# First layer: modulation by feature tiles, and four projection tiles accumulated in four banks as its weights arrive

## What is computed

```python
shift_l, scale_l, gate_l = jnp.split(jax.nn.silu(c) @ w_mod + b_mod, 3, axis=-1)
shift_c, scale_c, gate_c = jnp.split(jax.nn.silu(c_ctx) @ w_mod + b_mod, 3, axis=-1)
u_lat = rmsnorm(h_lat, norms[layer]) * (1 + scale_l[:, None]) + shift_l[:, None]
u_ctx = rmsnorm(h_ctx, norms[layer]) * (1 + scale_c) + shift_c
...
cq, ckv, k_rope, mq, mk, mv, mo, gates, z = split_cols(u @ w_in, EVEN_SPLITS)
```

## Time and profile before

| what | us |
|---|---|
| median of three timed runs | 4002.68 |
| lowest and highest of them | 4002.27, 4006.74 |
| the profiled execution | 3993.9 |
| its span, first to last instruction | 3992.1 |
| PE busy in the span | 3902.0 |
| DVE, ACT, POOL busy | 1857.0, 975.5, 933.2 |
| mean granted TensorE clock | 0.993 |

### The profile page before, as it was taken

The page is one execution under the profiler, slowest core; times in us unless marked ns, Lnnn a source line. Parts: engine busy times, 40 slices in busy tenths (PEclk is TensorE's granted clock), DMA queues, the critical chain, the costliest instruction groups (busy, mean ns, idle before and its releaser), DMA issues. The chain is left out here.

```text
span 3992.1 us, 48487 instructions
## 1 busy us (share of the span) xinstructions
PE 3902.0 (98%) x18394; PEld 2416.5 (61%) x18394; DVE 1857.0 (47%) x3855; ACT 975.5 (24%) x1838; POOL 933.2 (23%) x992
## 2 busy tenths in 40 slices
PE   7999999999999999989999999999999999999998
PEld 3688997777558468567544565656544444444447
DVE  3227775676343366746466322222566452223134
ACT  4223332333124311145325311111123010000000
POOL 0005775001111111133222111122232122222223
PEclk9999999999999999999999999999999999999999
DMA  5320003111211121132131112113243211111113
GB/s 215 129 89 10 8 9 68 42 47 48 90 35 69 50 64 49 59 110 80 64 98 50 57 37 80 42 58 103 96 139 130 79 32 42 47 48 43 42 45 104
DMA packets 113718, 270.25 MB, mean 68 GB/s; under 512 B 15624, under 2 KB 45178, under 8 KB 112399
## 3 DMA queue, kind: packets, MB, share of 16 engines
q1 hardware_dynamic: 106512, 251.81, 19.1%
q0 software_dynamic: 5920, 13.25, 1.3%
q10 hardware_dynamic: 1056, 2.10, 0.1%
HBM read 218.53 MB, written 50.87 MB: 67 GB/s over the span
## 5 line engine op out<-in xcount | busy, mean ns | idle before, releaser
L426 PE MATMUL upper_banks<-sbuf 128*128 128x512 f32 (+1 forms) x2016 | 771.5, 545 | 1.5 <-issue 1.1
L3325 PE MATMUL upper_banks<-sbuf 128*128 128x512 f32 x1400 | 613.7, 594 | 4.7 <-ACT sbuf L3602 3.1
L426 PEld LDWEIGHTS upper_banks<-sbuf 128*128 128x128 f32 x2016 | 382.4, 190 | 388.8 <-issue 373.5
L3325 PEld LDWEIGHTS upper_banks<-sbuf 128*128 128x128 f32 x1400 | 262.1, 190 | 315.1 <-issue 306.8
L2467 PE MATMUL gla_prod<-sbuf 128*128 128x512 f32 x560 | 247.6, 593 | 0.3 <-DVE sbuf L2499 0.3
L582 DVE TENSOR_TENSOR sbuf<-upper_banks,sbuf 128x512 f32<-128x512 f32 (+1 forms) x140 | 82.0, 586 | 283.1 <-PE upper_banks L426 282.5
L378 POOL TENSOR_TENSOR sbuf<-sbuf 128x512 f32<-128x512 f32 x36 | 47.1, 1307 | 655.5 <-DMA sbuf<-in_w_mlp_out 307.4
L2467 PEld LDWEIGHTS gla_prod<-sbuf 128*128 128x128 f32 x560 | 104.5, 192 | 119.9 <-issue 117.4
L1007 PE MATMUL mla_banks<-sbuf 128*128 128x128 f32 x1344 | 174.3, 278 | 2.5 <-DVE sbuf L1314 1.7
L1627 PE MATMUL mls_banks<-sbuf 128*128 128x512 f32 x392 | 175.1, 593 | 0.0
L1007 PEld LDWEIGHTS mla_banks<-sbuf 128*128 128x128 f32 x1344 | 162.1, 193 | 11.8 <-POOL sbuf L850 7.4
(11 more groups left out here) (569 smaller groups left out, 6635.7 us busy)
## 6 DMA issues: line engine op xcount, KB each, us to landing
sbuf<-in_l_w_in SPq DMA_DIRECT2D x59, 512.0 KB, 4.0
sbuf<-in_w_in SPq DMA_DIRECT2D x52, 512.0 KB, 4.2
sbuf<-in_w_mlp_out SPq DMA_DIRECT2D x40, 512.0 KB, 3.6
sbuf<-in_w_mlp_in SPq DMA_DIRECT2D x32, 512.0 KB, 3.6
sbuf<-in_l_w_mod SPq DMA_DIRECT2D x24, 512.0 KB, 5.2
scratch_gates<-sbuf SPq DMA_DIRECT2D x48, 256.0 KB, 2.0
sbuf<-in_l_w_mod SPq DMA_DIRECT2D x8, 1024.0 KB, 15.3
sbuf<-in_l_w_out SPq DMA_DIRECT2D x16, 512.0 KB, 4.1
```

What stands on the lines that cost most here:

```text
L426: last = nc.tensor.matmul(bank_of(n, c)[:, 0:wd], lw[:, k * P:(k + 1) * P], right_operand(c, base, tw, k, o, wd, to), start=k == 0 and c i ...
L3325: last = nc.tensor.matmul(pb, lw[:, k * P:(k + 1) * P], rhs, start=k == 0 and c in ("P1", "P2", "P5"), stop=k == 3, skip_group_check=True)
```

## The change

1. The modulation weights are cut in another way: column tile c holds 256 columns of shift and the 256 columns of scale for the same feature tiles 2c and 2c+1. So mod and gain of two feature tiles are complete after each column tile (`modulate(c)`).
2. SP loads two projection tiles before column tile 1 and two more before column tile 2 (t1, ckv0, ckv1, cq0), and H's late parts at the end.
3. In `modulation` ACT shifts feature tiles 0 to 5 (EARLY = 6) of the first third, and PE accumulates their products for four projection tiles in banks 0 to 3, between the column tiles. Feature tiles 6 and 7 are added in `mla_block` (chunks 0 to 3). The banks are now one tensor for both blocks.
4. The squares of the second third no longer start in `modulation`; all 16 late squares are in `mla_block`, with the evictions of chunks 0 and 1 in their middle. `late_sums` stands in chunk 2, ahead of its first matmul, `late_spread` in chunk 3 ahead of its last.
5. `mla_stream` is reordered: four tiles on the first third, then t1 and ckv0 by thirds, ckv1 and cq0, then the rest; the mod tiles start later and are denser.

```diff
-        w_next = [Memory.whole[0:P, base + i * D:base + (i + 1) * D] for i in range(2)]
+        w_next = [Memory.whole[0:P, base + i * D:base + (i + 1) * D] for i in range(4)]
...
             for c in range(NC):
...
+                if c < 2:
+                    load_first(2 * c)
+                    load_first(2 * c + 1)
...
-            act.wait_ge(h_late[0], 16)
-            for k in range(4):
...
+            for k in range(EARLY):
+                act.wait_ge(moded, k // 2 + 1)
+                act.wait_ge(lifted, k + 1)
+                for a, n, v in halves_of(0, 512):
+                    last = nc.scalar.activation(U[:, k, a:a + n], U[:, k, a:a + n], ACT.Identity, bias=mod[:, k, v:v + 1],
+                                                scale=gain[:, k, v:v + 1])
+                last.then_inc(normed, 1)
...
+            def products(kk, tiles):
+                pe.wait_ge(normed, kk + 1)
+                for t in tiles:
+                    if kk == 0:
+                        pe.wait_ge(w_first[t], 16)
+                    nc.tensor.matmul(banks[:, t, :], w_next[t][:, kk * P:(kk + 1) * P], U[:, kk, 0:512], start=kk == 0, stop=False)
+
+            pe.wait_ge(silued, 1)
+            columns(0)
+            pe.wait_ge(added, KD - 1)
+            pe.wait_ge(const_in, 48)
+            column_sums(nc, stat, total, ones, range(4)).then_inc(ssum, 1)
+            turn(0)
+            pe.wait_ge(rinvd, 1)
+            spread(nc, factor, rcol, ident, range(4)).then_inc(spreaded, 1)
+            for c in range(1, NC):
+                columns(c)
+                products(2 * c - 2, range(2))
+                turn(c)
+                products(2 * c - 1, range(2))
+                if c > 1:
+                    for kk in range(0 if c == 2 else 4, 2 * c):
+                        products(kk, range(2, 4))
...
             for k in range(1, KD):
                 add(k)
-            copy(1)
+            copy(0)
             dve.wait_ge(rooted, 1)
             nc.vector.reciprocal(rcol[:, 0:4], rcol[:, 0:4]).then_inc(rinvd, 1)
-            copy(2)
+            dve.wait_ge(in_sem, 64)
+            modulate(0)
             dve.wait_ge(spreaded, 1)
...
+            for k in range(5):
+                lift(k)
+            copy(1)
+            for k in range(5, KD):
+                lift(k)
+            modulate(1)
+            for c in range(2, NC):
+                copy(c)
+                modulate(c)
...
-        while m < 32 and ring >= (1 if m < 2 else 3 + 27 * (m // 2) // 16):
+        while m < 32 and ring >= (4 + 4 * (m // 2) if m < 4 else 12 + 17 * (m // 2 - 2) // 14):
...
-        late = [(512, 512, 4 + i) for i in range(4)] + [(1024, 256, i) for i in range(8)]
+        late = [(o, wd, i) for o, wd in thirds()[1:] for i in range(KD)]
+        adds_to = [sum(kk > 0 for _, _, kk in late[:i + 1]) for i in range(len(late))]
...
-                    for kk in range(KD):
+                    for kk in range(EARLY if n < 4 else 0, KD):
                         if t == 0:
-                            pe.wait_ge(normed, KD * (o // 512) + kk + 1)
+                            pe.wait_ge(normed, KD * (o // 512) + kk + 1 - EARLY)
+                        if n == 2 and kk == EARLY:
+                            late_sums()
+                        if n == 3 and kk == KD - 1:
+                            late_spread()
...
             def late_sums():
-                pe.wait_ge(hadd, 11)
+                pe.wait_ge(hadd, adds_to[-1])
...
             shift(0)
-            for i in range(12):
+            for i in range(len(late)):
                 o, wd, kk = late[i]
-                act.wait_ge(h_late[1 if o == 512 else 2], 16)
-                if i >= 2:
-                    act.wait_ge(hadd, i - 1 - (i - 2 >= 4))
-                nc.scalar.activation(hs[:, i % 2, 0:wd] if o == 512 or kk else total[:, o:o + wd], H[:, kk, o:o + wd],
-                                     ACT.Square).then_inc(hsq, 1)
...
+                act.wait_ge(h_late[2 if o == 1024 else kk // 4], 16)
+                if i >= 3:
+                    act.wait_ge(hadd, adds_to[i - 2])
+                nc.scalar.activation(hs[:, i % 2, 0:wd] if kk else total[:, o:o + wd], H[:, kk, o:o + wd], ACT.Square).then_inc(hsq, 1)
+                if i == KD - 1:
+                    evict(0)
+                    evict(1)
```

More of the change, by code:

```diff
@@ L126, in halves_of, with modulation @@
     return [(0, NCTX, 1), (NCTX, w - NCTX, 0)] if o == 0 else [(o, w, 0)]
-def modulation(nc, name, io, mod, gain, U, H, rcol, ones, ident, eps, at, h_late, w_first):
+EARLY = 6
+def modulation(nc, name, io, mod, gain, U, H, rcol, ones, ident, eps, at, h_late, w_first, banks):
     NC = NB = 4
@@ L192, in _, with columns @@
             nc.scalar.activation(rcol[:, 0:4], stat[:, 0:4], ACT.Sqrt, bias=eps, scale=1.0 / D).then_inc(rooted, 1)
-            act.wait_ge(h_late[0], 16)
-            for k in range(4):
[L195 to L199, removed]
+            for k in range(EARLY):
[5 more added lines that the diff above has]
+                last.then_inc(normed, 1)
         @block.tensor
         def _(pe):
[L203 to L210, removed]
+            def columns(c):
                 if c >= 2:
@@ L218, in _, with turn @@
                 last.then_inc(mm_done, 1)
[L219 to L228, removed]
+            def turn(c):
+                pe.wait_ge(copied, c + 1)
+                for a in range(4):
+                    last = nc.tensor.matmul(col[:, 4 * c + a, :], part[:, c % 2, a * P:(a + 1) * P], sel[:], start=True, stop=True)
+                last.then_inc(turned, 1)
+            def products(kk, tiles):
[20 more added lines that the diff above has]
+                        products(kk, range(2, 4))
         @block.vector
@@ L796, in _ @@
             sp.dma_start(tab[64:P, :], io["rope"]).then_inc(tab_in, 16)
-            for t in range(2, NW - 1):
+            for t in range(4, NW - 1):
                 load_w(t)
@@ L942, in _ @@
                     chunk(n)
[L943 to L946, removed]
                 if o == 1024 and (what, j) == ("cq", 1):
@@ L1112, in shift @@
                 o, wd = thirds()[c]
-                for k in range(KD):
+                for k in range(0 if c else EARLY, KD):
                     if c:
@@ L1139, in _ @@
                     nc.scalar.activation(rcol[:, 4:TT], banks[:, 5, 260:256 + TT], ACT.Sqrt, bias=eps, scale=1.0 / D).then_inc(hroot, 1)
+                if n >= 2 and (what != "mod" or j % 2):
+                    evict(n)
+                if n == 2:
+                    shift(1)
+                    act.wait_ge(zeroed, 1)
+                    act.wait_ge(misc_in, 16 * 9)
+                    nc.scalar.activation(sc[:, :, 0:2], cc.rearrange("p (a b) -> p a b", b=2), ACT.Silu).then_inc(silued, 1)
                 if n == 3:
-                    shift(1)
                     shift(2)
@@ L1272, in _ @@
             last.then_inc(zeroed, 1)
-            for i in range(12):
+            for i in range(len(late)):
                 o, wd, kk = late[i]
-                if i == 4:
+                if kk == 0:
                     continue
@@ L4826, in lower_layers @@
         mod, mod1, gain = s.sb("mod", [P, 3 * KD, 2]), s.sb("mod1", [P, 3 * KD, 2]), s.sb("gain", [P, KD, 2])
-        h_late, w_first = [s.sem(f"h_late{i}") for i in range(3)], [s.sem(f"w_first{i}") for i in range(2)]
-        modulation(nc, "mod0", io, mod, gain, U, H, rcol, ones[:], ident[:], eps[:], 7680, h_late, w_first)
+        h_late, w_first = [s.sem(f"h_late{i}") for i in range(3)], [s.sem(f"w_first{i}") for i in range(4)]
+        first = ExitStack()
+        banks = first.enter_context(nc.psum_tensor("mla_banks", [P, 8, 512], F32))
+        modulation(nc, "mod0", io, mod, gain, U, H, rcol, ones[:], ident[:], eps[:], 7680, h_late, w_first, banks)
         mv, ma, mn, mf, ao = scratch("mv", [T, 512]), scratch("ma", [8, T]), scratch("mn", [8, T]), scratch("mf", [8, T]), scratch("ao", [512, T])
         ahead, ahead_at = [s.sem(f"ahead{i}") for i in range(2)], Memory.top + KV_WEIGHTS
-        o_out = mla_block(nc, "mla", U, H, io, mv, ma, mn, mf, ao, mod, gain, rcol, mod1, ones, ident, eps[:], ahead, h_late, w_first)
+        o_out = mla_block(nc, "mla", U, H, io, mv, ma, mn, mf, ao, mod, gain, rcol, mod1, ones, ident, eps[:], ahead, h_late, w_first, banks)
+        first.close()
         retire_semaphores()
```

80 lines of the change are left out of this document (36 added, 44 removed).

## The result

The changed kernel takes 4013.97 us (median of ten runs, 4011.64 to 4015.56) against 4003.6 us of the kernel before (ten runs, 4001.33 to 4006.74).

The account below looks back on a forecast made before the run. PE, 98% busy, bounds the kernel; its head before 61.09 is nearly the only slack. Milestone 77.5 against 74.0 (+3.5) plus 2.7 at mv3 gives +6.2, so 4008.9 us from 4002.7; range 4001 to 4015.

Parts of the forecast that it names:

- The loads: Modulation weights: column tile 1 lands at 22.8, tile 2 at 30.3, tile 3 at 35.4; H's late parts by 43.
- The products in the modulation: Column tiles, turns and 20 products follow without waiting for data; PE ends at 53.9, the stage for all engines at 54.2.
- The price of the low clock: PE at column tile 1, from 22.8: 3.7 us at the low clock, costing 1.8.
- Rival A: Low clock holds through the whole stretch 22.8 to 31; milestone 82, sum +10.7, 4013.5 us; chance 0.22.
- What is late next: Behind the modulation's barrier: late squares and adds end at 68.9, so PE stands 9.8 us before the late sums.
- The clock after the stall: Behind the wait at the late sums: 3.7 us at half rate, costing 1.9, bounds 1.3 to 3.4.
- The ring's load: At mv3, whose weights reuse mv2's slot: 2.7 us stall, bounds 0 to 2.9, 1.7 more if the clock falls.
- Rival B: Late sums are in time behind the barrier; milestone 66.4, with the ring -5, 3997.6 us; chance 0.08.

Follow-up runs that it names:

- ring: Changed kernel with the last two pairs of mod tiles one chunk later in the stream, so mv3's slot is freed earlier; 4009.60 us, ratio 1.0018 to the kernel before.
- early0: Changed kernel with EARLY = 0, no products between the column tiles; 4019.09 us, ratio 1.0039 to the kernel before.
- squares: Changed kernel with the 16 late squares and 14 adds moved back ahead of the barrier, into the modulation block; 3998.87 us, ratio 0.9988 to the kernel before.
- memsets: Changed kernel with VectorE's five memsets of the second block moved behind the late adds; 4012.66 us (one run).
- warm: Changed kernel with 11 idle matmuls of 512 columns where PE waits for the late sums; 4007.64 us, ratio 1.0010 to the kernel before.
- early2: Changed kernel with EARLY = 2, only 8 of 24 products between the column tiles; 4012.25 us, ratio 1.0024 to the kernel before.

## Why the prediction was right, point by point

**The loads** came as predicted, but the changed kernel's own profile can't show it: there PE reaches column tiles 1 and 2 at 23.09 and 31.12 with other work in hand, and waits for neither. Other executions show the landings. In ring, whose loads are the same, PE waits for tile 1:

```profile
22.80 3.64 PE L217 MATMUL mla_banks<-sbuf 128*32 128x512 f32 x16 [2.47 <-DMA sbuf<-in_l_w_mod]
```

That is the 22.8 of the prediction, and in early0 it waits for tile 2 until 30.47 (30.3 predicted).

**The products in the modulation:** PE is done at 54.2 (53.9 predicted) and ACT starts behind the barrier at 54.52 (54.2). The price of the low clock, 1.8, was right in size, but not for the reason given. The prediction had PE arrive at column tile 1 "having mostly stood"; in this profile it had worked without a pause since 14.11, and all of that at half rate: sums, turn and spread took 1.87, 1.84 and 2.05 us, where ring has 1.05, 1.03 and 1.14 for them. (In ring PE did stand for 2.47 us, as the prediction had it, and the tile took 3.64.) Column tile 1 followed in 3.58, and only the products at 26.60 ran at the full rate (1.98 for four records). The granted clock reads 1.00 all this while, so here the durations decide and not that view. For the same reason it is the 1.98 at 26.60 that speaks against Rival A, in which the low clock holds to 31. The Trainium skill's rule on loop structure ("TensorE: Matmul & The Clock Gate", section "Loop structure matters more than you think"), as the prediction read it, would have sent PE cold between the column tiles. The trace doesn't agree with that reading from 26.6 on, since the products fill the waits for the DMA. It agrees with the rule in the kernel without them (early0, clock 0.64 in that stretch).

**What is late next:** the wait at the late sums was predicted at 9.8 and is 9.84, its end at 68.9 and is 69.3. The cause is shown by its removal (squares, 14 us) and by one of its parts (memsets, 1.7).

**The clock after the stall** is the first term that was mis-sized: 1.9 predicted with bounds of 1.3 to 3.4, and 4.0 in the profile of the changed kernel (against warm); 3.6 in memsets and 2.7 in ring, which is inside the bounds. I took the 3.7 us of low clock from the earlier trace rows. There PE had been idle for less than 4 us; here it had stood for 9.8 and then began with six tiny matmuls (twelve records), and the clock stayed low for 8 us of its work. Which of the two made the difference was not tested.

**The ring's load:** the stall was 2.9 (2.7 predicted, bound 2.9). I had the fall of the clock in it only as a possible 1.7; in this profile it did fall, and cost 2.8. This is the second mis-sized term, and in three of the six executions with that stall it was nothing. Together the two are 4.9 of the 6.1 us between the predicted +6.2 and the +12.3 of the trace; the barrier and small pieces are the rest.

**The verdict:** the direction and the mechanisms held; the size was short. The +12.3 of the trace lies above the prediction's own upper bound of +11, the timed +10.4 inside it. The forecast of less than 8 us did not hold, because the clock behind each stall took a second price, up to 41% of the long stall and up to 95% of the short one. The time of 4013.97 is also outside the 4004 to 4012 that the prediction gave to its own mechanism. It lies in the stated range only because that was drawn over **Rival A** (4013.5), whose mechanism did not happen: that part is luck. A time more than 8 us slower by the forecast's own terms had been given 0.06. **Rival B**, in time as the change intends, is what squares shows: its milestone of 65.77 against the 66.4 that I had given it.

## What to carry to other kernels

Moving work of the bound engine ahead of a barrier only pays if the next thing that it waits for moves too; list what stood under the work that was moved (here 12 squares under 16 matmuls) and ask what covers it now. An engine that stands idle ahead of a barrier while its own work waits behind it (ACT for 16 us) is the sign to look for. In a ring of buffers, a tile that reuses the slot of the tile just finished is a stall of one load's latency, less the work in between (here 4.2 less 1.3), and counting slots between the two finds it without running anything.

## What was new about the hardware

A stall of TensorE can cost more than its length. Behind 9.84 us of idling the granted clock stayed at 0.50 for 8 us of work, and 4.0 us were lost; behind the same stall in ring (9.85) it was 2.7, and behind 8.15 in memsets 3.6. Eleven matmuls whose result nobody reads, put into the stall, kept the clock at 1.00 and took back the 4.0.

The stall at mv3 was there in six of the profiled executions, with about the same length and the same dense work around it:

| kernel | stall, us | next 64 records, us |
|---|---|---|
| changed | 2.94 | 10.20 |
| squares | 2.88 | 10.17 |
| warm | 2.92 | 8.85 |
| memsets | 3.00 | 7.41 |
| early2 | 2.92 | 7.41 |
| early0 | 2.73 | 7.41 |

In the first three the granted clock fell to 0.50 at the stall; in the last three it reads 1.00 throughout. So the price of the same stall was 2.8, 1.4 or nothing, and the length of the stall doesn't order them. What decides is open.

In the first microseconds the granted clock of these profiles can't be relied on. It reads 1.00 from 14 to 27, while the same eight records of the turn take 1.84 us in the changed kernel and 1.03 in ring.
